# Splitting a ring of eight gathered-row buffers into three for U rows and five for V rows, with five rows instead of eight issued ahead of a stage's end

## The reference, cut to what matters

```python
def chunk(xc):                                     # 128 tokens at a time, 8 chunks
    ...                                            # scores, top 16, top 16 of the pairs
    expert = ia * PEER_KEYS + ib                   # (128 tokens, 8 heads, 16 picks)
    g = jax.nn.softmax(best_s, axis=-1)
    u = u_tab[expert]
    a = jax.nn.gelu(jnp.einsum('cd,chkd->chk', xc, u), approximate=False)
    coeff = g * a
    return jnp.einsum('chk,chkd->cd', coeff, v_tab[expert])
```

## Time and profile before

| | us |
|---|---|
| median of 3 launches | 3813.63 (3812.23 to 3817.93) |
| the profiled launch, its own time | 3823.41 |
| its span in the profile | 3821.6 |
| busy PE / DVE / ACT / POOL | 2960 / 2483 / 1299 / 1414 |
| POOL, gathers of U rows alone | 331, of V rows alone 331 |
| POOL, gathers of pairs | 693 |

### The profile page before, as it was taken

How to read it: one execution, slowest core, us unless ns; L and a number is a source line. 1 busy time by engine, 2 the same in 40 slices (tenths; PEclk the granted TensorE clock), 3 DMA queues, 4 the chain that set the end, 5 groups by cost and what they waited for, 6 DMA issues and landing times.

```text
span 3821.6 us, 34961 instructions
## 1 busy us (share of the span) xinstructions
PE 2960.3 (77%) x8920; PEld 1529.5 (40%) x8920; DVE 2483.2 (65%) x5699; ACT 1299.2 (34%) x3333; POOL 1413.9 (37%) x1367
## 2 busy tenths in 40 slices
PE   8797967984887499989779787777878787765665
PEld 6645523331444255545444343333333333322222
DVE  0311217786777377667527878877887887788765
ACT  1212311221111144434334534544443444344333
POOL 0000003443576366657523333333333333333332
PEclk9898878997898699999889999999989999999999
DMA  7835145777998999999899999999999999999998
GB/s 289 274 134 198 56 204 188 241 266 257 352 339 323 327 367 341 352 332 347 331 357 350 402 410 415 414 407 421 402 406 420 416 413 396 421 411 413 419 414 351
DMA packets 274454, 1297.10 MB, mean 339 GB/s; under 512 B 27888, under 2 KB 63088, under 8 KB 180464
## 3 DMA queue, kind: packets, MB, share of 16 engines
q0 software_dynamic: 195120, 1073.83, 71.8%
q1 hardware_dynamic: 74384, 203.74, 14.3%
q10 hardware_dynamic: 4752, 17.30, 1.2%
HBM read 1231.07 MB, written 63.70 MB: 339 GB/s over the span
## 4 chain that ended last, share of the span: by engine, by line
DMA 31%; issue 8%; DVE 4%; PE 4%; ACT 3%; POOL 0%; POOLq 0%; DVEq 0%; SPq 0%; ACTq 0%
DMA s_ring<-peer_uv,s_expert 17%; DMA e_more_slots<-peer_uv,s_expert 10%; PE e_acc L503 3%; PE e_product L1860 1%; DVE e_part L427 1%; DMA e_more_slots<-peer_v,s_expert 1%; DMA next_h<-e_h 1%; DMA e_h<-norm_ffn_row 1%; DMA s_scratch<-norm_final_row 1%; DVE s_ring L394 1%; ACT L341 0%; ACT s_diagonal L324 0%; ACT s_gate L343 0%; DVE s_dots L394 0%; DVE e_top_at L1697 0%
## 5 line engine op out<-in xcount | busy, mean ns | idle before, releaser
L503 PE MATMUL e_acc<-s_ring,s_diagonal 128*128 128x512 f32 (+1 forms) x2168 | 913.9, 551 | 384.2 <-ACT s_diagonal L324 357.9
L394 DVE CUSTOM_DVE_ANT_0 s_ring<-s_ring,e_x_copy 128x1024 f32<-128x1024 f32 x548 | 667.0, 1217 | 221.1 <-DMA s_ring<-peer_uv,s_expert 213.3
L503 PEld LDWEIGHTS e_acc<-s_ring,s_diagonal 128*128 128x128 f32 x2168 | 404.1, 202 | 954.2 <-ACT s_diagonal L324 585.1
L278 POOL DMA_INDIRECT s_ring<-peer_uv,s_expert x462 | 438.1, 948 | 790.9 <-DVE e_part L427 544.1
L278 POOL DMA_INDIRECT s_ring<-peer_u,s_expert x331 | 375.0, 1133 | 466.2 <-DVE s_expert L1797 235.5
L278 POOL DMA_INDIRECT s_ring<-peer_v,s_expert x325 | 368.6, 1134 | 346.8 <-PE e_acc L503 98.5
L503 PE MATMUL e_acc<-e_more_slots,s_diagonal 128*128 128x512 f32 (+1 forms) x948 | 378.8, 526 | 148.0 <-ACT s_diagonal L324 137.3
L341 ACT ACTIVATE s_dots<-s_dots 128x1 f32<-128x1 f32 x704 | 142.2, 202 | 960.5 <-DVE s_dots L394 959.7
L324 ACT ACTIVATE s_diagonal<-s_ident,s_gate 128x128 f32<-128x128 f32 x949 | 371.3, 399 | 229.2 <-PE e_acc L503 105.5
L278 POOL DMA_INDIRECT e_more_slots<-peer_uv,s_expert x231 | 217.5, 942 | 404.5 <-DVE e_part L427 264.4
L394 DVE CUSTOM_DVE_ANT_0 s_ring<-s_ring,s_x 128x1024 f32<-128x1024 f32 x245 | 299.4, 1222 | 95.4 <-DMA s_ring<-peer_u,s_expert 63.9
(11 more groups left out here) (233 smaller groups left out, 3644.5 us busy)
## 6 DMA issues: line engine op xcount, KB each, us to landing
w_in_kept<-w_in SPq DMA_DIRECT2D x8, 1104.0 KB, 8.6
w_in_gained<-w_in_kept SPq DMA_DIRECT2D x8, 1104.0 KB, 10.3
p_w_in<-w_in_gained SPq DMA_DIRECT2D x8, 1104.0 KB, 20.2
f_w_big<-w_mem_kv SPq DMA_DIRECT2D x4, 2048.0 KB, 19.2
f_w_big<-peer_w_q_t SPq DMA_DIRECT2D x2, 4096.0 KB, 17.9
peer_scores<-f_stage_s SPq DMA_DIRECT2D x16, 512.0 KB, 5.1
e_mem_scores<-mem_scores SPq DMA_DIRECT2D x2, 4096.0 KB, 14.6
e_mem_values<-mem_values SPq DMA_DIRECT2D x2, 4096.0 KB, 24.9
```

Source lines behind the costliest of these rows:

```text
L278: pool.indirect_dma_start(out=to, out_offset=None, in_=table, in_offset=bass.IndirectOffsetOnAxis(ap=self.expert[c % PICK_BUFFERS][:, k:k ...
L394: dve.tensor_tensor_reduce(row, row, x[:, :], 1.0, 0.0, ALU.mult, ALU.add, self.dots[:, k:k + 1]).then_inc(self.u_used, 1)
L503: last = pe.matmul(self.acc[:, at:to], self.diagonal[:, made % DIAGONALS, :], row[:, at:to], start=(n == group[0]), stop=(n == group[-1]))
```

## The change

U and V rows get slots of their own from place 22 on: 3 for U, 5 for V. A U row then waits for the U row six places back, a V row for the V row ten places back. At place 640, where only V rows follow, all eight slots go to V rows in the order of their last use; at 648 the four new ones come in front; at 662 the slots are paired anew, in the order of the later of the two last uses. `ahead` becomes `until + 5`.

```diff
+U_SLOTS = 3
...
+            if n == LEAD:
+                lanes = {"u": free[:U_SLOTS], "v": free[U_SLOTS:]}
+            if n == self.stages[-1][0]:
+                lanes["v"] = sorted(range(RING), key=lambda slot: last_in[slot])
             if n == wide_from:
-                free = list(range(RING, WIDE_RING)) + free
-            slot = free.pop(0)
-            free.append(slot)
+                lanes["v"] = list(range(RING, WIDE_RING)) + lanes["v"]
+            if n == PAIRS_AT:
+                doubles = sorted(range(0, WIDE_RING, 2), key=lambda slot: max(last_in[slot], last_in[slot + 1]))
+                both = [slot + i for slot in doubles for i in range(2)]
+                lanes = {"u": both, "v": both}
+            lane = lanes[kind] if n >= LEAD else free
+            slot = lane.pop(0)
+            lane.append(slot)
...
     def ahead(self, until):
-        return min(until + RING, len(ROWS))
+        return min(until + RING - U_SLOTS, len(ROWS))
```

## The result

| | kernel before | changed kernel |
|---|---|---|
| median in this comparison | 3814.43 (3810.85 to 3817.93, 6 runs) | 3835.85 (3833.18 to 3845.47, 6 runs) |
| ratio, 95% interval | | 1.0057 [1.0042, 1.0071] |
| the profiled launch, own time | 3823.41 | 3845.47 |
| its span | 3821.6 | 3843.7 |

The forecast was 3831.0, in a range of 3808 to 3857. The same code, timed again beside other kernels, had 3834.18 against 3804.07 (1.0091). The changed kernel repeats to 2 us; it is the kernel before whose median was 3814 here and 3804 to 3806 in the three later comparisons, which ran on three different chips (the record doesn't name the chip of the first). So the cost is 21 to 30 us by medians.

What follows compares the result with a forecast made beforehand. Each stage has its own limit: stage 3 DMA at 0.99, stage 2 often late rows. Terms 0 + 3.5 + 3.5 + 0 + 3.8 + 6.6 + 0 = +17.4 us take the median from 3813.6 to 3831.0; range 3808 to 3857.

Steps and rivals of the forecast that it cites:

- Stage 0: Stage 0: shorter U window costs 0 us, as rows lead their use; V relief is worth nothing there.
- U window, stage 1: Stage 1: six U places instead of eight cost up to 2.4 us in each disturbed moment; 3.5 us, bounds -1 and +17.
- Stage 2 body: Stage 2: U-slot waits lose 10 us, V-slot relief gains 6.5; net +3.5 us, bounds -20 and +20.
- Ahead into stage 1: Places 155 to 157 issued after the barrier: 0 us, bounds -1.2 and +2.
- Ahead into stage 2: Places 305 to 307 behind the barrier: first scores 12.4 us late, stream three rows behind; 3.8 us, bounds 0 and +12.
- Ahead into stage 3: Places 645 to 647 behind the barrier, PE late at 647 and 6.6 us late at 651; 6.6 us, bounds +3 and +10.
- Re-pairing: Place 662: second and third pair wait for later places but are not used sooner anyway; 0 us, bound +3.
- the U lane binds in every burst: Rival, slower still: both window terms at their upper bounds, +47 us, 3861; chance 0.12.
- Boundaries only: Rival, slower: U lane never binds, only stage 2 and 3 boundary terms lost, 10.4 us, 3824; chance 0.20.
- V slots were the brake: Rival, faster: stage 2's V-slot waits hold up POOL; a third reaching the pace gives -19 us, 3795; chance 0.13.
- Hidden: Rival, no change: PE's work makes up for late rows, tables finish sooner, windows free; about +3 us, 3817; chance 0.15.
- second rival: Skill page's case: gather 3.2 us, U slot trip 4.5 us, so both U window terms are nothing; no separate chance given.

Runs made afterwards that it cites:

- the two runs of one window each: Kernel before with slots split 3 U and 5 V only at places 308 to 639 (1.0041), or only at 158 to 299 (1.0043); eight ahead.

## Why the prediction was right, and what in it was wrong

The direction held, and so did the size: +17.4 us forecast, +21.4 by the first medians and +30 by the second, both in the range. But the sum was less right than it looks.

- **Stage 0: 0.** It held. DVE waits 1.6 us for U rows (1.3 before), though POOL's waits turned there too, from PE to DVE's dot products (112.1 us).
- **U window, stage 1: 3.5 (bounds -1 and +17). This step failed**: it is 15.3 us by the traces and 16 by time. The prediction said "it fits, with the old eight places (9.8 us) and with six", from a trip of 5.9 us, taken from the first gather of the kernel. In stage 1 a gather takes 6.2 to 6.4 us from the start of its issue to its landing (medians; changed kernel and the kernel split in stage 1 alone), and with one ring no less (6.4 to 6.6, second profile of the kernel before). With 1.22 us of use and 0.1 us to POOL that is a trip of 7.5 to 7.7 us: eight places, 9.8 us, cover it with 2 us to spare; six, 7.3 us, do so no longer. And the trip left out POOL's own pace. In a burst DVE goes on every 1.25 us (1.22 for a U, 1.28 for a V row), while POOL needs some 1.6 us for each gather, so each further place comes later than the one before and only the stock bridges it. Of the 38 rows that DVE waited for in stage 1 of the changed kernel, 36 were issued 0.3 us behind the gather before them, with their own slot free for 1.0 us or more: POOL was late with them because it had stood still for a U slot some places earlier. It did that 9 times after the stage's start, for 43.4 us (71.0 less 27.6), where the kernel before had 6 such waits and 10.8 us (47.0 less 36.2). Here are POOL and DVE in order of time, in the changed kernel: POOL stands for 6.62 us until DVE, which itself waited 5.97 us for the next x, has used a U row; then it issues one gather behind the other. The slot used by DVE at 1121.48 is refilled by the gather at 1123.81 and used again at 1133.19, 11.7 us later.

```profile
1116.44 1.80 POOL L289 DMA_INDIRECT s_ring<-peer_u,s_expert  x1 [6.62 <-DVE s_dots L405]
1118.54 1.18 POOL L289 DMA_INDIRECT s_ring<-peer_v,s_expert  x1 [0.30 <-issue]
1120.03 1.75 POOL L289 DMA_INDIRECT s_ring<-peer_u,s_expert  x1 [0.30 <-issue]
1122.08 1.43 POOL L289 DMA_INDIRECT s_ring<-peer_v,s_expert  x1 [0.30 <-issue]
1123.81 0.94 POOL L289 DMA_INDIRECT s_ring<-peer_u,s_expert  x1 [0.30 <-issue]
1125.05 3.13 POOL L289 DMA_INDIRECT s_ring<-peer_v,s_expert  x1 [0.30 <-issue]
1128.49 1.78 POOL L289 DMA_INDIRECT s_ring<-peer_u,s_expert  x1 [0.31 <-issue]
```

```profile
1121.48 1.21 DVE L405 CUSTOM_DVE_ANT_0 s_ring<-s_ring,s_x 128x1024 f32<-128x1024 f32 x1
...
1133.19 1.23 DVE L405 CUSTOM_DVE_ANT_0 s_ring<-s_ring,s_x 128x1024 f32<-128x1024 f32 x1 [0.19 <-DMA s_ring<-peer_u,s_expert]
```

  So the price doesn't lie in disturbed gathers alone, as I had it; "seven such moments" were 38 waits. That both the missing 2 us of reserve and POOL's pace are at work is read from these rows; no run changed POOL's pace. And the cover held only in part: the statistics' wait fell from 12.9 to 4.0 us.
- **Stage 2 body: 3.5 (bounds -20 and +20). Also mis-sized**: 15.8 us by the traces, widely spread, and 15.6 by the ratio of the timed run of that part alone (14.5 by medians). Here the gain of 6.5 us from V slots is what failed. The prediction names the reason itself ("a U row that waits holds the V row behind it too") and then doesn't use it: 110 us of V waits went, 116 us of U waits came. That leaves the loss, for which I had 10 us, at some 15. The gain rested in part on the mixed waits of the earlier trace rows told of above.
- **Ahead into stage 1: 0.** The change of block came out 1.7 us shorter, just outside the bound of -1.2 (0.7 us with one ring, 2.1 with the split).
- **Ahead into stage 2: 3.8.** Right in size (3.1). The first scores came at 1289.99, 33.9 us after the stage's first load (at 1256.09); in the kernel before it was 1277.96 - 1256.76 = 21.2 us, so they are 12.7 us late, where I had 12.4. PE had waited for 305 and 307, and the stream was some 3 us behind by place 320:

```profile
1276.35 2.05 PE L514 MATMUL a_acc<-s_ring,s_diagonal 128*128 128x512 f32 x2 [16.08 <-DMA s_ring<-peer_v,s_expert]
1288.15 2.04 PE L514 MATMUL a_acc<-s_ring,s_diagonal 128*128 128x512 f32 x2 [9.76 <-DMA s_ring<-peer_v,s_expert]
1289.99 3.62 PE L1442 MATMUL a_scores<-mla_k_t_rest,a_q_mla 96*128 96x512 f32 x4
```

  **The sum missed** the 4.5 us that the same edit gives back just before, at the end of stage 1.
- **Ahead into stage 3: 6.6 (3 to 10).** Right: 7.7 by the traces, 6 by time, at the very place foretold, with PE waiting at 647. The chain of waits of the changed kernel names it:

```profile
1917.25 45.34 DMA s_ring<-peer_v,s_expert
```

- **Re-pairing: 0.** Nothing shows a cost; it wasn't tried by itself.

So the windows cost 31 us where I had 7, and the boundaries about 5 net (3 to 6 by time) where I had 10.4. That is nearer to the rival in which *the U lane binds in every burst*, 37 us of windows, than to my own case. The forecast is close by luck: two errors of opposite sign, and a first comparison that showed the smaller cost. *Boundaries only* fell with the two runs of one window each. *V slots were the brake* fell with the view by kind of gather: they were, and freeing them moved the brake. *Hidden* fell with the 7 us of PE's wait.

Of my signs, the length of stage 1, PE's wait at 647 and the late scores came as said. DVE's wait for U rows rose too (71.2 against 62.1), but the second profile of the kernel before has 76.8, so this sign shows nothing by itself. DVE's wait for V rows in stage 2 was to fall below 47.7 and rose to 59.6. Most of that is the stage's start and not the short lane: with one ring and five ahead it is 60.7, with the split and eight ahead 54.1.

The page's figure, by which both window terms would be nothing (an estimate of 3.2 us a gather from the Trainium skill, page DMA: Bandwidth & Descriptors, section Anatomy of one DMA), doesn't hold here: in a stage with a DMA share of 0.90 a gather takes 6.2 to 6.4 us to its landing by the median, and the one in the rows above is used 9.4 us after its issue began. The prediction calls this case its second rival; with both window terms at nothing it is the first, *boundaries only*.

## What to carry to other kernels

Where two kinds of rows are issued in one order by one queue, a split of the buffers made the smaller share the window for both here, and the larger share's extra buffers stood idle; look for the waits by kind of gather, to see whether a relief moves on or only changes its name. Size a buffer's round trip in the stage in which it is to hold, not by the first transfer, and set beside it the pace at which the issuing engine can refill. And a queue of small gathers that starves at a stage's start was helped by cutting the big loads beside it into pieces (-0.26%), while being less far ahead cost 6 us.

## What the hardware showed that I had not expected

- A gather of 512 KB took 45 us to land beside table packets of 39.7 KB on average; with table packets of 6.4 KB the third gather behind the barrier was used 15.5 us after its issue, at a total rate of 398 GB/s against 426, and the kernel was 0.26% faster.
- POOL's issue of one gather isn't of one length: 0.94 us at best, 3.13 in the rows above, a mean of 1.13 to 1.16 us in stage 2 and 1.29 to 1.35 in stage 1. In a burst, DVE takes a U and a V row in 2.5 us while POOL needs 2 x (1.3 + 0.3) = 3.2 us to issue them, so DVE lives from the stock, of which the split took two places.
- After 7 us without work PE's next four matmuls (two of 512 and two of 256 columns) took 2.90 us, twice as long as the next four, at a granted clock of 0.50 (1.2 GHz) against 1.00.
